# First pass of the linear attention: scores placed two levels behind their scalings, a third pair of scaled operands, older work of PE spread, two factors by a bias

## The reference, cut to what matters

```python
def step(S, inp):                       # one chunk, one direction
    qc, kc, vc, gc = inp
    bc = jnp.cumsum(gc, axis=2)
    o = jnp.einsum('bhcd,bhde->bhce', qc * jnp.exp(bc), S)
    diff = bc[:, :, :, None, :] - bc[:, :, None, :, :]
    decay = jnp.exp(jnp.where(causal, diff, -jnp.inf))
    att = jnp.einsum('bhid,bhijd->bhij', qc, decay * kc[:, :, None, :, :])
    o = o + jnp.einsum('bhij,bhje->bhie', att, vc)
    bl = bc[:, :, -1:, :]
    S = (jnp.exp(bl[:, :, 0, :])[..., None] * S
         + jnp.einsum('bhcd,bhce->bhde', kc * jnp.exp(bl - bc), vc))
    return S, o
of, sf = gla_chunk_scan(q, k, v, gf, s0f)
ob, sb = gla_chunk_scan(rev(q), rev(k), rev(v), rev(gb), s0b)
o = (of + rev(ob))
```

## Time and profile before

| | |
|---|---|
| median of 3 runs | 2951.65 us (2949.37 to 2954.92) |
| the profiled execution's own time | 2951.81 us |
| its span, first to last instruction | 2949.7 us |
| mean granted clock of PE | 0.979 |
| PE busy | 2802.5 us, 95% |
| DVE busy | 1488.7 us, 50% |
| ACT busy | 1264.2 us, 43% |
| POOL busy | 159.3 us, 5% |
| stretch from the first `kh` scaling to the last placing of the first pass | 1768.41 to 1943.14 us |

### The profile page before, as it was taken

The page is one execution under the profiler, slowest core; times in us unless marked ns, Lnnn a source line. Parts: engine busy times, 40 slices in busy tenths (PEclk is TensorE's granted clock), DMA queues, the critical chain, the costliest instruction groups (busy, mean ns, idle before and its releaser), DMA issues. The chain is left out here.

```text
span 2949.7 us, 39699 instructions
## 1 busy us (share of the span) xinstructions
PE 2802.5 (95%) x15243; PEld 2451.2 (83%) x15243; DVE 1488.7 (50%) x2277; ACT 1264.2 (43%) x2054; POOL 159.3 (5%) x260
## 2 busy tenths in 40 slices
PE   5999999899999999999999987877999999999998
PEld 3878887789999999999897767766789999999997
DVE  4255665555545445444313558875555554445444
ACT  5144444444344434333324655654454443334333
POOL 0000000000000000000000009820000000000000
PEclk8999999999999999999999998899999999999999
DMA  7633224333444344344224430024334344444433
GB/s 268 211 124 108 94 94 139 111 114 120 123 128 143 122 128 150 122 124 126 67 57 143 129 113 8 1 78 158 107 122 124 121 149 128 128 123 148 127 123 112
DMA packets 299493, 355.13 MB, mean 120 GB/s; under 512 B 20086, under 2 KB 242748, under 8 KB 298332
## 3 DMA queue, kind: packets, MB, share of 16 engines
q1 hardware_dynamic: 291760, 333.10, 36.1%
q10 hardware_dynamic: 5580, 12.29, 1.2%
q0 software_dynamic: 2016, 7.86, 0.7%
HBM read 337.88 MB, written 15.34 MB: 120 GB/s over the span
## 5 line engine op out<-in xcount | busy, mean ns | idle before, releaser
L1258 DVE TENSOR_TENSOR p_lo<-p_raw,p_hi 128x1024 fp32r<-128x1024 f32 x507 | 619.5, 1223 | 691.2 <-ACT p_hi L746 690.9
L746 ACT ACTIVATE p_hi<-p_raw 128x1024 fp32r<-128x1024 f32 x507 | 533.1, 1052 | 558.9 <-DMA p_raw<-mlp_w 407.0
L2012 PE MATMUL ps<-hm_hi,p_hi 128*128 128x384 f32 x1536 | 516.4, 336 | 4.8 <-DVE hm_lo L1279 4.0
L2012 PE MATMUL ps<-hm_hi,p_lo 128*128 128x384 f32 x1536 | 516.5, 336 | 0.0
L2012 PE MATMUL ps<-hm_lo,p_hi 128*128 128x384 f32 x1536 | 515.0, 335 | 0.0
L1951 PE MATMUL ps<-p_hi,hid_hi 128*128 128x512 f32 x1152 | 363.3, 396 | 3.5 <-DVE p_lo L1258 3.5
L1951 PE MATMUL ps<-p_lo,hid_hi 128*128 128x512 f32 x1152 | 357.7, 392 | 0.0
L1951 PE MATMUL ps<-p_hi,hid_lo 128*128 128x512 f32 x1152 | 357.0, 391 | 0.0
L948 ACT ACTIVATE relu<-ps 128x384 f32<-128x384 f32 x192 | 94.4, 492 | 541.0 <-PE ps L2012 541.0
L1483 DVE TENSOR_TENSOR sqr<-relu 128x384 f32<-128x384 f32 x192 | 107.2, 558 | 391.6 <-ACT relu L948 391.6
L2012 PEld LDWEIGHTS ps<-hm_hi,p_hi 128*128 128x128 f32 x1536 | 289.0, 188 | 14.1 <-DVE hm_lo L1279 4.5
(11 more groups left out here) (229 smaller groups left out, 3735.6 us busy)
## 6 DMA issues: line engine op xcount, KB each, us to landing
p_raw<-mlp_w SPq DMA_DIRECT2D x384, 512.0 KB, 3.9
mod_p<-mod_w SPq DMA_DIRECT2D x80, 512.0 KB, 4.0
p_raw<-gla_w_in SPq DMA_DIRECT2D x56, 512.0 KB, 3.6
p_raw<-gla_w_out SPq DMA_DIRECT2D x24, 512.0 KB, 3.4
mod_w<-mod_w SPq DMA_DIRECT2D x8, 1024.0 KB, 19.2
p_raw<-ab_w_in SPq DMA_DIRECT2D x14, 512.0 KB, 5.3
p_raw<-ab_w_out SPq DMA_DIRECT2D x12, 512.0 KB, 3.7
p_raw<-ab_w_out SPq DMA_DIRECT2D x24, 256.0 KB, 3.9
```

Source lines behind the costliest of these rows:

```text
L746: nc.scalar.activation(p_hi[s][:, :, 0:width], p_raw[s][:, :, 0:width], ACT.Copy).then_inc(pan_hi, 1)
L1258: V.tensor_tensor(p_lo[s][:, :, 0:width], p_raw[s][:, :, 0:width], p_hi[s][:, :, 0:width].bitcast(F32), ALU.subtract).then_inc(pan_lo, 1)
L2012: mm = M.matmul(ps[:, b, 0:GN], w[s][:, c, :], x[:, c, :], start=(c == 0 and x is hi and w is p_hi), stop=(c == DC - 1 and w is p_lo))
```

## The change

The order of the first pass changes, with a buffer pair more and two of POOL's gaps done by ACT:

- `xx` gets a third pair; the pair is chosen by the running number of the level over all tiles (`turn = NL * a + level`), and S (M at the last level) waits for the scores three levels back.
- DVE places a level's scores after the M scaling two levels later (`place_behind`), so the last two levels of a tile are placed in the next tile, after M0 and M1.
- `k1` moves from the tile's start to behind level 2, on ACT and DVE.
- The state step moves from level 5, ahead of M6, to behind `q1`, with its wait for `ob_ready`.
- PE's update is split in two heads after the scores of level 1 and two after level 2; the output in head 0 after level 3, head 1 after level 4, heads 2 and 3 after level 5.
- ACT's `o_take` moves from behind factor M5 to behind factor M6, ahead of factor `q1`; the store of the context's backward state moves with its wait to tile a = 2.
- The gaps of `k0` and `q1` go from POOL. ACT takes these factors from the cumulated gates, one head (128 x 128) at a time, with the reference as a bias, from a small tile `ref_s` that two ACT copies fill ahead of the pass.

The waits of `gram`, the copy of the diagonal and `khn` on ACT, and the closings after level 1 stay as they are.

```diff
--- before.py
+++ after.py
@@ -183,6 +183,7 @@
...
     xx = [[at(f"xx{i}{x}", [P, GH, P], F32, w + 16384 + 4096 * i + 2048 * x) for x in range(2)] for i in range(2)]
+    xx.append([at(f"xx2{x}", [P, GH, P], F32, w + 36864 + 2048 * x) for x in range(2)])
     og = [at(f"og{i}", [P, D], F32, o) for i, o in enumerate((w + 45056, RS))]
@@ -199,6 +200,7 @@
...
     dec = at("dec", [P, 2 * TILES, GH], F32, RS + 8864)
+    ref_s = at("ref_s", [P, 2 * TILES, GH], F32, RK + 3104)
     rs4 = at("rs4", [P, TILES, 2, GH], F32, RK + 6304)
@@ -594,6 +596,7 @@
...
         NL = len(LEVELS)
+        XX = len(xx)
@@ -602,14 +605,14 @@
...
             for a, tile in enumerate(TURNS):
-                if tile != 1:
-                    out.append(("k1", tile, 0))
                 for level in range(NL):
...
                         out += closing(TURNS[a - 1])
+                    if level == 2 and tile != 1:
+                        out.append(("k1", tile, 0))
                 if tile:
@@ -625,15 +628,11 @@
...
                     out.append(("f", tile, level))
-                elif kind in ("k0", "q1"):
-                    out.append((kind, tile, 0))
             return out
...
         def gap_user(kind, tile, level):
-            if kind in ("k0", "q1"):
-                return factor_at[(kind, tile, level)]
             return factor_at[("S" if kind == "f" and LEVELS[level] > 1 else "M", tile, level)]
@@ -663,11 +662,6 @@
...
                 out = dd[r % 4]
-                if kind in ("k0", "q1"):
-                    b = bc_b if kind == "q1" else bc_f
-                    ref = tot_b[:, tile].unsqueeze(2) if kind == "q1" else b[:, tile, :, P - 1:P]
-                    nc.gpsimd.tensor_tensor(out[:], b[:, tile], ref.broadcast_to([P, GH, P]), ALU.subtract).then_inc(d_ready, 1)
-                    continue
                 n = LEVELS[level]
@@ -1116,6 +1110,8 @@
...
             act.dma_start(st[1][:], io["state_bwd"][0, 0].rearrange("h k v -> k h v")).then_inc(st_in, 16)
+            nc.scalar.activation(ref_s[:, 0:TILES, :], bc_f[:, :, :, P - 1], ACT.Copy, scale=1 / GATE_NORM)
+            own(nc.scalar.activation(ref_s[:, TILES:2 * TILES, :], tot_b[:], ACT.Copy, scale=1 / GATE_NORM))
             nc.scalar.activation(dec[:, 0:TILES, :], bc_f[:, :, :, P - 1], ACT.Exp, scale=1 / GATE_NORM)
@@ -1131,9 +1127,10 @@
...
                 elif kind in ("q1", "k0"):
-                    r = gap_at[(kind, tile, 0)]
-                    act.wait_ge(d_ready, r + 1)
-                    nc.scalar.activation(out, dd[r % 4][:], ACT.Exp, scale=-s).then_inc(e_ready, 1)
+                    b, ref = (bc_b, ref_s[:, TILES + tile]) if kind == "q1" else (bc_f, ref_s[:, tile])
+                    for h in range(GH):
+                        last = nc.scalar.activation(out[:, h], b[:, tile, h], ACT.Exp, scale=-s, bias=ref[:, h:h + 1])
+                    last.then_inc(e_ready, 1)
                 else:
@@ -1156,8 +1153,6 @@
...
             for a, tile in enumerate(TURNS):
-                if tile != 1:
-                    exp_factor("k1", tile)
                 for level in range(NL):
@@ -1173,11 +1168,13 @@
...
                             exp_factor(*x)
-                    if level == 5 and a:
-                        o_take(a - 1)
-                    if level == 5 and a == 1:
+                    if level == 2 and tile != 1:
+                        exp_factor("k1", tile)
+                    if level == 2 and a == 2:
                         act.wait_ge(st_ready, 1)
                         act.dma_start(io["new_state_bwd"][0, 0].rearrange("h k v -> k h v"), st[0][:]).then_inc(st_out, 16)
+                    if level == 6 and a:
+                        o_take(a - 1)
                 if tile:
@@ -1598,11 +1595,10 @@
...
                 if kind in ("S", "M"):
-                    if kind == "S" or LEVELS[level] == 1:
-                        reader = 8 * a + 1 + level - 2 if level >= 2 else 8 * a - 1 - (level == 1)
-                        if reader > 0:
-                            dve.wait_ge(gram_ready, reader + 1)
-                    out, x = xx[level % 2][0 if kind == "S" else 1][:], (gk if kind == "S" else gq)[:, tile]
+                    turn = NL * a + level
+                    if (kind == "S" or LEVELS[level] == 1) and turn >= XX:
+                        dve.wait_ge(gram_ready, 8 * ((turn - XX) // NL) + 2 + (turn - XX) % NL)
+                    out, x = xx[turn % XX][0 if kind == "S" else 1][:], (gk if kind == "S" else gq)[:, tile]
                 elif kind == "k1":
@@ -1645,28 +1641,31 @@
...
             dve.wait_ge(dec_ready, 1)
+            def place_behind(turn):
+
+                if turn >= 0:
+                    place(*divmod(turn, NL))
+
             for a, tile in enumerate(TURNS):
-                if tile != 1:
-                    scale("k1", tile)
                 for level in range(NL):
...
                     scale("M", tile, level)
-                    if level:
-                        place(a, level - 1)
-                    elif a:
-                        place(a - 1, NL - 1)
+                    place_behind(NL * a + level - 2)
                     if level == 1 and a:
...
                             scale(*x)
-                    if level == 5 and a:
-                        dve.wait_ge(ob_ready, a)
-                        if a == 2:
-                            dve.wait_ge(st_in, 16)
-                        state_step(1, TURNS[a - 1])
+                    if level == 2 and tile != 1:
+                        scale("k1", tile)
                 if tile:
                     scale("q1", tile)
-            place(TILES - 1, NL - 1)
+                if a:
+                    dve.wait_ge(ob_ready, a)
+                    if a == 2:
+                        dve.wait_ge(st_in, 16)
+                    state_step(1, TURNS[a - 1])
+            place_behind(NL * TILES - 2)
+            place_behind(NL * TILES - 1)
             for x in closing(TURNS[-1]):
@@ -2133,15 +2132,17 @@
...
-            def update(n, tile):
-
-                pe.wait_ge(khn_ready, n + 1)
-                if n:
-                    pe.wait_ge(st_ready, n)
-                for h in range(GH):
+            def update(n, tile, h0=0, h1=GH):
+
+                if h0 == 0:
+                    pe.wait_ge(khn_ready, n + 1)
+                    if n:
+                        pe.wait_ge(st_ready, n)
+                for h in range(h0, h1):
                     last = M.matmul(psf[:, 5 * 512 + DV * h:5 * 512 + DV * (h + 1)], khn[n % 2][:, h, :],
                                     gv[:, tile, DV * h:DV * (h + 1)], start=True, stop=True)
-                last.then_inc(upd_ready, 1)
+                if h1 == GH:
+                    last.then_inc(upd_ready, 1)
@@ -2180,12 +2181,12 @@
...
                     pe.wait_ge(xt_ready, factor_at[("M", tile, level)] + 1)
-                    x = xx[level % 2]
+                    x = xx[(NL * a + level) % XX]
                     gram(a, 1 + level, x[0] if LEVELS[level] > 1 else gk[:, tile], x[1])
-                    if level == 1 and a:
-                        update(a - 1, TURNS[a - 1])
-                    if level in (2, 3) and a:
-                        att_out(a - 1, 2 * (level - 2), 2 * (level - 1))
+                    if level in (1, 2) and a:
+                        update(a - 1, TURNS[a - 1], 2 * level - 2, 2 * level)
+                    if level in (3, 4, 5) and a:
+                        att_out(a - 1, *((0, 1), (1, 2), (2, 4))[level - 3])
                     if level == 6 and tile != 1:
```

## The result

The changed kernel takes 2990.09 us (median of 4 runs, 2989.59 to 2992.0) against 2953.28 us; the ratio is 1.0128 with a 95% interval of 1.0116 to 1.0141. That is slower, by 37 us; 2984 was forecast.

The account below looks back on a forecast made before the run. No engine full; a loop of waits sets the pace, 20.02 us a tile. 16.23 work, 3.86 and 4.02 stalls and 0.5 small ones make 24.6; in all +32.5 us on 2951.8 gives 2984 us, range 2970 to 2998.

Parts of the forecast that it names:

- Both chains: In a tile, S1 waits for ACT's diagonal copy, 3.86 us, and q1 for the older tile's output, 4.02 us.
- Rival (a): Only one of the two new waits appears: 31 us off, 2953 us, no difference from before; chance 0.05.
- rival (b): DVE's own work is the pace, both chains done when DVE reaches S1 and q1: 2921 us; chance 0.06.
- The four pieces: Factors k0 and q1 on ACT as four 128x128 instructions each: about 1.2 us, where one 128x512 took 0.60.
- The gain side: DVE's old waits over eight tiles go: 13.9 us before placings, 8.1 before kh; at most 3.8 a tile.
- Tile 0: First tile, paced by POOL's gaps: M6 scaled at 1780.49 as before, next S0 at 1781.7.
- PE's state behind a restart: PE keeps up even with scores of levels 0 and 1 at the low clock level, 1.70 us each.
- six tiles: The tiles after tile 1, at 24.6 us each: 147.6 us, to 1951.05.
- tile 1: One closing less, half the output matmuls, a plain state copy: 21.7 us, to 1803.45.
- the entry: Ahead of the pass: two ref_s copies cost about 0.5 us, k1 at the head (0.5) goes, so nothing.
- rival (c): PE at the low level also in level 5 and the output: +2.5 us in seven tiles, 3002 us; chance 0.07.
- The low level at the start of the tiles: PE restarts at 1.2 GHz for the diagonal score: 0.90 us in all tiles; sum 7 us smaller without it.

Follow-up runs that it names:

- e1: The change with level 5 placed in its own tile, behind q1, and level 6 behind M0 of the next tile: 2957.38 us, ratio 1.0027.
- e2: The change with ACT's factor q1 ahead of its copy of the older tile's output: 2965.05 us, ratio 1.0057.
- e3: The change with DVE's state step back ahead of q1: 2977.46 us, ratio 1.0100.
- e8: The change with factor q1 ahead of the output's copy, output one level earlier on PE, every level placed one level behind its scaling: 2930.50 us.
- e12: e8 with one output head behind the scores of each of levels 2 to 5: 2927.73 us, ratio 0.9928.

## Why the prediction was right

Its steps against the tile shown above, one of the shorter ones, t from S0 at 1880.09 and s from S1 at 1885.85:

| step | forecast | measured |
|---|---|---|
| placing of level 5 | t + 1.20 | 1.21 |
| `gram(a, 0)` | t + 2.07 | 1.98 |
| ACT's copy to `att` | t + 4.06 | 4.15 |
| S1 | t + 5.68 | 5.76 |
| k0 scaled | s + 1.97 | 2.00 |
| S2 | s + 3.33 | 3.36 |
| placing of level 4 | s + 11.97 | 11.99 |
| score of level 5 on PE | s + 11.63 | 11.89 |
| ACT's copy of the output | s + 14.45 | 14.71 |
| q1 scaled | s + 16.61 | 16.90 |

- **Both chains** are shown, each by an experiment that cuts it alone: e1 for the diagonal, e2 and e3 for the output. Rival (a), one wait only, and rival (b), DVE's pace, fell with the profile after: both waits are there, 34.9 and 29.8 us. e8 to e12 come near to the state that (b) described, at 2928 to 2933 us for its 2921.
- **The four pieces** took 1.23 us for 1.2.
- **The gain side**: 21 us of old waits went as said, 13.9 to 0.8 and 8.1 to 0.
- **Tile 0** ended as forecast, next S0 at 1781.84 for 1781.7. POOL's relief was of no use behind it, since POOL then stood 9 to 10 us a tile.
- **The term that was too small** is PE's state behind a restart. The last placing ended 38.3 us later than before (its end at 1982.07) and not 32.5. From S0 to S0 six tiles took 152.0 us (1804.15 to 1956.15) for 147.6, the last 0.7 more, tile 1 0.6 and the entry 0.1. I had let the low level last up to two scores and had PE done with level 4 and head 1 at s + 11.6, in time for level 5. Even in the tile of the table it was 0.3 us late (11.89 for 11.63). In three of the six tiles, those with 4.9 us of wait ahead of q1, the low level went on into the update, and in two of them into the score of level 2 (PE's timeline after, the tile from 1851.86):

```profile
1865.52 1.91 PE L2142 MATMUL ps<-gv,khn 128*128 128x256 f32 x4
1867.23 1.35 PE L2156 MATMUL ps<-xx,xx 128*128 128x128 f32 x8
```

Four update records take 1.91 us here and 1.03 at the high level, PE reaches the score of level 5 a microsecond later than in the tile of the table, and the wait ahead of q1 is 4.9 us in place of 4.0; the two such tiles with a full state step take 25.95 and 26.09 us, the others some 24.9. This is rival (c) in part: the low level reached further than forecast, but not level 5 and the output, which ran at the high level. That `qh` scalings stood 25.3 us apart and not 24 to 25 comes from it too. Why the low level ends earlier in one tile and later in the next is open.

The low level at the start of the tiles came as forecast, 2.08 us at `gram(a, 0)` behind 4.65 us of idle. The rule that the prediction cites for it (the Trainium skill, "TensorE: Matmul & The Clock Gate", section "HAM oscillation — how this bites in real kernels") would have it in every round, and the trace of the change agrees from the third tile on. In e2, with 2.53 us of idle, some tiles restarted at the high level (1.16 us).

## What to carry to other kernels

Putting a step later, as the placings here, relieves its wait only if nothing behind it in another engine's queue is needed sooner: walk each engine's order and look for a wait on something that the waiting engine's own partner has released just before. Work that was moved may have been the cover of another wait; say what stands there when it has gone. With the copies of the diagonal and of the output freed the kernel gained 0.6 to 0.7% (e8 to e12), where the change as a whole lost 1.3%. Of the ideas in the title the second level of distance, the third pair and the factors by a bias were each worth nothing that could be measured then. Each was taken out by itself, never all three. If that holds for them together, the gain lies in the others: `k1` later, PE's older work spread, the state step behind `q1`, and the factor q1 ahead of the output's copy. No run takes these apart.

## What the runs showed of the hardware

- A restart at the low level could last longer than the work between two standings: in the tile from 1851.86 the diagonal score ran at 1856.12, PE stood 3.78 us, and the granted clock was 0.50 from 1855 to 1867, through the next two scores and half of the update.
- The idle time just ahead of a score does not by itself tell its level. Behind 4.65 us of idle `gram(a, 0)` took 2.07 to 2.08 us in six tiles of the change; behind 2.53 (e2) it took 1.16 to 1.94, behind 1.77 (e1) 1.16 to 2.01.
- With shorter standings PE was at the high level for more of the time: over seven tiles the granted clock was 0.78 in the change, 0.94 in e8 and 1.00 in e12, with PE's longest wait 4.7, 2.8 and 1.7 us.
- Four exps of 128x128 with a bias from memory ran in 1.23 to 1.24 us, one in 0.36 on average; the exp of 128x512 in 0.60.
